# Branch output projection after the fourth unit of the first mixing gate, its first two tiles side by side, and the gated sum split behind all gates

## The chip, the cores and the metric

The kernel runs on one core of a Trainium2 chip. The metric is the device time of one launch in microseconds. Five engines work beside each other and meet at semaphores: TensorE (PE in the profile: matmuls; PEld is its weight loading), VectorE (DVE), ScalarE (ACT), GpSimd (POOL) and SyncE (SP), which here only issues DMAs. Each engine takes its instructions in the order in which the program gives them.

## The reference

Two layers of a hybrid decoder run over 592 tokens (512 prompt tokens, 16 meta tokens, and 8 running sequences of 8). One layer computes, in float32:

```python
proj = rmsnorm(x, ln_g) @ w_in                    # 1024 -> q,k,v,z_a,x_b,z_b,g_a,g_b
o_a = group_norm(retention(q, k, v), gn_g) * silu(z_a)       # 2048 wide, 4 heads
o_b = rglru(causal_conv(x_b)) * silu(z_b)                    # 1536 wide
merged = sigmoid(g_a) * (o_a @ w_a) + sigmoid(g_b) * (o_b @ w_b)
x = x + merged @ w_o
```

After both layers x is normalised once more. The outputs are y and the new retention, convolution and RG-LRU states.

## The kernel before

**Tiles.** Activations lie transposed: a tile is 128 features on the partitions by all 592 tokens. In the last layer the 16 meta tokens are no longer needed, and its later stages work on 576. A product is computed for the two halves of the tokens (296 or 288 columns) in two PSUM banks. Every float32 product is three matmuls (`three`, L1657 to L1659): both operands are split into a high part, which is rounded to the format of the fast matmul, and the low rest; hi·hi, hi·lo and lo·hi are summed. The high part is made by ScalarE as a copy (`w_hi`, `ob_hi`, `xn_hi`), the low part by VectorE as the difference (`w_lo`, `ob_lo`, `xn_lo`).

**Weights.** They come as "units" of 128x1024 (512 KB, eight 128x128 blocks) through a ring of four slots. For each unit SyncE waits until the unit four places earlier is done on TensorE (`unit_done`) and issues the DMA to `w_raw`; ScalarE makes `w_hi` (`split_hi`, L464), VectorE makes `w_lo` in the place of `w_raw` (`split_lo`, L472). `split_hi(ph, i)` and `split_lo(ph, i)` treat the unit three places (`AHEAD`) behind unit i. PSUM banks are a ring of four as well: a job waits for `bank_free` of its bank, and whoever reads the bank sets it free.

**Stages of a layer**, with names as in the code: R (four retention heads, each with its part of `o_a @ w_a` summed into `acc`), L (the RG-LRU branch, whose last work on VectorE are three scans that give the tiles of `ob`, 12 in all), GA (8 units: the projections of the gate g_a), GB (8 units: those of g_b), B (`o_b @ w_b`: 12 units, 8 output tiles m with 12 input tiles k each, 1.5 units to a tile), O (8 units: `merged @ w_o`).

**Around the change.** The order on each engine is written out by hand. In GA and GB ScalarE reads each bank with a tanh into `sg` (`tanh_g`, L934); VectorE multiplies `acc` by the first gate (L1552). Between GA and GB come the splits of `ob` (L990 and L1557). In B VectorE reads each bank itself: it multiplies it by the second gate in `sg` (L1577), adds the tile to `acc` (L1581), and the split of this sum into `xn_hi` (L1002, ScalarE) and `xn_lo` (L1567, VectorE), the operands of O, follows tile by tile. B doesn't read `xn_hi` and `xn_lo`, GA and GB do. O begins with `project_first`, which takes the input tiles k of the sum as they become ready: the first three for one output tile only, and then two output tiles at a time. POOL loads the old x (`xT`, 2368 KB, L688) once `ob` is finished; O adds it. The copy to `xg_hi` in O prepares the next layer.

## Time and profile before

| | us |
|---|---|
| median of 3 runs | 1926.42 (1926.24 to 1926.42) |
| the profiled execution, whole | 1926.77 |
| its span, first to last instruction | 1924.9 |
| TensorE busy in the span | 1904.5 (99%) |
| VectorE, ScalarE, GpSimd busy | 1187.7, 760.9, 267.5 |
| granted TensorE clock, mean | 0.999 of full speed |

The profile's times are from its span's start. L with a number is a line of the kernel before. "Busy" of TensorE contains some overlap of neighbouring matmuls: one is shown with about 0.30 us and the next begins 0.135 us after it. The stages of the first layer that the change touches lie from 736 us (GA begins) to 945 us (in O), and those of the second from 1683 to 1890 us.

### The profile page before, as it was taken

The numbers are of one execution on the slowest core, as the hardware profiler recorded it, in microseconds if no ns is written. First come the engines' busy times: TensorE is split into PE (matmuls) and PEld (weight loads), VectorE is DVE, ScalarE is ACT, GpSimd is POOL, SyncE is SP. The second block draws the span as 40 slices with busy tenths as digits, with TensorE's granted clock in tenths as the row PEclk, the third lists the DMA queues.
The fourth block names the chain that finished last, engine by engine and source line by source line (L and its number), as shares of the span: only waits on it lengthen the run. The fifth ranks groups of instructions, "written<-read, shape, count | busy, mean of one in ns | idle before, by whom it ended". The sixth has DMA issues, their size and how long they took to land.

```text
span 1924.9 us, 32032 instructions
## 1 busy us (share of the span) xinstructions
PE 1904.5 (99%) x13112; PEld 1782.1 (93%) x13112; DVE 1187.7 (62%) x2008; ACT 760.9 (40%) x1181; POOL 267.5 (14%) x375
## 2 busy tenths in 40 slices
PE   8999999999999999999999999999999999999998
PEld 7889898898899999999998988988988999999997
DVE  8775665665766887424487656657557678763345
ACT  5432322323327776422344223233123377754223
POOL 2221120120231200000022201202102422000000
PEclk9999999999999999999999999999999999999999
DMA  6435534453443433322254435534444533342222
GB/s 216 133 117 164 169 136 127 161 174 111 146 149 93 114 99 113 113 77 77 88 172 156 139 127 171 171 114 146 164 127 135 163 102 110 92 138 77 87 79 82
DMA packets 105857, 246.99 MB, mean 128 GB/s; under 512 B 10830, under 2 KB 51262, under 8 KB 105326
## 3 DMA queue, kind: packets, MB, share of 16 engines
q1 hardware_dynamic: 78590, 149.71, 24.9%
q0 software_dynamic: 26976, 95.22, 14.9%
q8 instruction: 104, 1.70, 0.4%
q14 instruction: 43, 0.35, 0.1%
q10 hardware_dynamic: 144, 0.00, 0.0%
HBM read 186.07 MB, written 49.12 MB: 122 GB/s over the span
## 4 chain that ended last, share of the span: by engine, by line
PE 85%; DVE 5%; ACT 4%; DVEq 2%; DMA 1%; ACTq 1%; issue 1%; SPq 0%
PE bank L1657 21%; PE bank L1659 20%; PE bank L1658 20%; PE bank L1727 4%; PE bank L1729 4%; PE bank L1728 4%; PE last L1745 1%; PE last L1727 1%; PE last L1729 1%; PE last L1728 1%; PE sums L1852 1%; PE sums L1854 1%; PE sums L1856 1%; PE bank L1908 1%; PE sums L1763 1%
## 5 line engine op out<-in xcount | busy, mean ns | idle before, releaser
L1657 PE MATMUL bank<-xn_hi,w_hi 128*128 128x296 f32 (+1 forms) x2432 | 726.7, 299 | 0.2
L1659 PE MATMUL bank<-xn_lo,w_hi 128*128 128x296 f32 (+1 forms) x2432 | 722.3, 297 | 0.0
L1658 PE MATMUL bank<-xn_hi,w_lo 128*128 128x296 f32 (+1 forms) x2432 | 721.5, 297 | 0.0
L1657 PEld LDWEIGHTS bank<-xn_hi,w_hi 128*128 128x128 f32 x2432 | 457.3, 188 | 6.6 <-issue 4.3
L1658 PEld LDWEIGHTS bank<-xn_hi,w_lo 128*128 128x128 f32 x2432 | 457.7, 188 | 1.1
L1659 PEld LDWEIGHTS bank<-xn_lo,w_hi 128*128 128x128 f32 x2432 | 456.8, 188 | 0.0
L472 DVE TENSOR_TENSOR w_lo<-w_raw,w_hi 128x1024 fp32r<-128x1024 f32 x245 | 300.3, 1228 | 186.2 <-ACT w_hi L464 179.3
L464 ACT ACTIVATE w_hi<-w_raw 128x1024 fp32r<-128x1024 f32 x245 | 257.8, 1055 | 353.8 <-DMA w_raw<-in_w_units 349.3
L1657 PE MATMUL bank<-oa_hi,w_hi 128*128 128x296 f32 (+1 forms) x512 | 153.7, 300 | 0.0
L1658 PE MATMUL bank<-oa_hi,w_lo 128*128 128x296 f32 (+1 forms) x512 | 151.9, 297 | 0.0
L1659 PE MATMUL bank<-oa_lo,w_hi 128*128 128x296 f32 (+1 forms) x512 | 151.7, 296 | 0.0
L1657 PE MATMUL bank<-ob_hi,w_hi 128*128 128x296 f32 (+1 forms) x384 | 113.9, 297 | 0.0
L1658 PE MATMUL bank<-ob_hi,w_lo 128*128 128x296 f32 (+1 forms) x384 | 113.9, 297 | 0.0
L1659 PE MATMUL bank<-ob_lo,w_hi 128*128 128x296 f32 (+1 forms) x384 | 113.8, 296 | 0.0
L1727 PE MATMUL bank<-w_hi,xn_hi 128*128 128x512 f32 x256 | 100.8, 394 | 0.7 <-DVE rot_k L1191 0.7
L1729 PE MATMUL bank<-w_lo,xn_hi 128*128 128x512 f32 x256 | 100.8, 394 | 0.0
L1728 PE MATMUL bank<-w_hi,xn_lo 128*128 128x512 f32 x256 | 100.7, 393 | 0.0
L1657 PEld LDWEIGHTS bank<-oa_hi,w_hi 128*128 128x128 f32 x512 | 96.3, 188 | 3.9 <-issue 3.9
L1658 PEld LDWEIGHTS bank<-oa_hi,w_lo 128*128 128x128 f32 x512 | 96.3, 188 | 0.0
L1659 PEld LDWEIGHTS bank<-oa_lo,w_hi 128*128 128x128 f32 x512 | 96.3, 188 | 0.0
L606 POOL DMA_DIRECT2D out_ret_s<-S x64 | 46.0, 721 | 326.5 <-DVEq L1142 181.4
L781 ACT ACTIVATE zz<-bank 128x296 f32<-128x296 f32 (+1 forms) x64 | 26.6, 415 | 133.3 <-PE bank L1659 132.7
(293 smaller groups left out, 3069.0 us busy)
## 6 DMA issues: line engine op xcount, KB each, us to landing
w_raw<-in_w_units SPq DMA_DIRECT2D x215, 512.0 KB, 3.6
S<-in_state_ret POOLq DMA_DIRECT2D x64, 512.0 KB, 4.7
out_ret_s<-S POOLq DMA_DIRECT2D x64, 512.0 KB, 6.3
w_raw<-in_w_units SPq DMA_DIRECT2D x66, 256.0 KB, 3.3
vst<-v_scr SPq DMA_DIRECT2D x8, 512.0 KB, 4.0
out_ret_p<-Sp POOLq DMA_DIRECT2D x8, 512.0 KB, 5.7
v_scr<-vtok_hi SPq DMA_DIRECT2D x16, 160.0 KB
dec<-in_decay POOLq DMA_DIRECT2D x9, 264.0 KB, 5.0
```

The lines of the kernel that those rows point to most:

```text
L464: act.activation(w_hi[:, n % RING, :], w_raw[:, n % RING, :], ACT.Copy).then_inc(unit_hi, 1)
L472: dve.tensor_tensor(w_lo[:, n % RING, :], w_raw[:, n % RING, :], w_hi[:, n % RING, :].bitcast(f32), SUB).then_inc(unit_lo, 1)
L606: pool.dma_start(dst, S[:, s, :, :]).then_inc(s_out[s], 16)
L781: act.activation(zz[:, i - 8, a:b], psum_of("R", name)[:, 0:b - a], ACT.Tanh, scale=0.5)\
L1657: pe.matmul(ps, w_hi[:, slot, cols], x_hi, start=first, stop=False)
L1658: pe.matmul(ps, w_lo[:, slot, cols], x_hi, start=False, stop=False)
L1659: return pe.matmul(ps, w_hi[:, slot, cols], x_lo, start=False, stop=last)
L1727: pe.matmul(ps, left_hi, right_hi, start=first, stop=False)
L1728: pe.matmul(ps, left_lo, right_hi, start=False, stop=False)
L1729: return pe.matmul(ps, left_hi, right_lo, start=False, stop=last)
L1745: ins = pe.matmul(o_last[at:at + QUAD, :], qz[:, c, b * QUAD:b * QUAD + QUAD], S[:, s, c, :], start=(n < 4 and c == 0), stop=(n >= 4 and c ...
L1763: return pe.matmul(to[:, :], kst[rows, b // 4, c * P:c * P + P], vst[rows, b // 4, :], start=True, stop=True)
```

## The change

The units now come in the order GA (4 units: g_a tiles 0 to 3), B (12 units), GB (12 units: g_a tiles 4 to 7, then g_b), O. The array of weights in memory stays as it is, and `stored` maps one order to the other.

- TensorE: B begins after the fourth unit of GA. Its output tiles 0 and 1 are computed side by side: for each k, both halves of both tiles, in four banks at once. Units are waited for when their first block is needed.
- ScalarE: the 12 copies `ob_hi` stand behind the third tanh of GA, with the fourth tanh and one weight split behind the first four copies. In B ScalarE copies each bank to `sg`. In GB it writes the tanh to a new buffer `tg` of two tiles. The eight copies `xn_hi` wait for the end of GB.
- VectorE: the differences `ob_lo` come straight behind the last scan and one weight split, and the gates of g_a behind them. In B it only splits weights. In GB it applies both gates and sums. The eight differences `xn_lo` stand behind all of that.
- POOL: the load of `xT` is behind B (its new place in memory is used by `ob` until then).

The diff, without the buffers' new places and the semaphores' names:

```diff
+        def stored(u):
+
+            at = u % UNITS_LAYER
+            first, middle, last = PH["B"].unit0, PH["GB"].unit0, PH["O"].unit0
+            if first <= at < middle:
+                return u + last - middle
+            return u - (middle - first) if middle <= at < last else u
...
-                    sp.dma_start(w_raw[:, u % RING, :], w_units[u]).then_inc(unit_in[u % RING], 16)
+                    sp.dma_start(w_raw[:, u % RING, :], w_units[stored(u)]).then_inc(unit_in[u % RING], 16)
...
-                pool.dma_start(xT[:, :, :].rearrange("p k t -> p (k t)"), x_in if l == 0 else x_scr[l - 1])\
-                    .then_inc(x_again, 16)
                 pool.dma_start(lp[:, :], packs[ds(l + 1, 1)].rearrange("o p w -> (o p) w")).then_inc(lp_in, 16)
...
+                pool.wait_ge(unit_done, l * UNITS_LAYER + PH["B"].after[1])
+                apart(pool)
+                pool.dma_start(xT[:, :, :].rearrange("p k t -> p (k t)"), x_in if l == 0 else x_scr[l - 1])\
+                    .then_inc(x_again, 16)
...
+                def tanh_ga(i):
 
                     for n, (a, b) in enumerate(cut(l)):
                         name = (("proj", i), n)
-                        if ph == "GB":
-                            act.wait_ge(ga_used, l * 16 + it * 8 + (i * 2 + n + 1))
-                        wait_job(act, ph, l, it, name)
+                        wait_job(act, "GA", l, 0, name)
                         apart(act)
-                        act.activation(sg[:, ds(it * 4 + i, 1), a:b].rearrange("p o t -> p (o t)"),
-                                       psum_of(ph, name)[:, 0:b - a], ACT.Tanh, scale=0.5)\
-                           .then_inc(freed(ph, name), 1)
-                        act.drain().then_inc(ga_ready if ph == "GA" else gb_ready, 1)
+                        act.activation(sg[:, i, a:b], psum_of("GA", name)[:, 0:b - a], ACT.Tanh, scale=0.5)\
+                           .then_inc(freed("GA", name), 1)
+                        act.drain().then_inc(ga_ready, 1)
+
+                def tanh_gb(it, i):
+
+                    j = it * 4 + i
+                    for n, (a, b) in enumerate(cut(l)):
+                        name = (("proj", i), n)
+                        if l * 12 + j >= 2:
+                            act.wait_ge(tg_used, (l * 12 + j - 2) * 2 + n + 1)
+                        wait_job(act, "GB", l, it, name)
+                        apart(act)
+                        act.activation(tg[:, j % 2, a:b], psum_of("GB", name)[:, 0:b - a], ACT.Tanh, scale=0.5)\
+                           .then_inc(freed("GB", name), 1)
+                        act.drain().then_inc(tg_ready, 1)
...
-                for ph in ("GA", "GB"):
-                    if ph == "GB":
-                        act.wait_ge(ob_ready, l * LT + LT)
-                        for k in range(LT):
-                            act.activation(ob_hi[:, k, first:], ob[:, k, first:], ACT.Copy).then_inc(obh_ready, 1)
-                    for it in range(0, 2):
-                        for i in range(4):
-                            if (ph, it, i) != ("GA", 0, 0):
-                                tanh_g(ph, it, i)
-                                split_hi(act, ph, l, it, i)
+                def high_ob(k):
+                    act.activation(ob_hi[:, k, first:], ob[:, k, first:], ACT.Copy).then_inc(obh_ready, 1)
+
+                for i in (1, 2):
+                    tanh_ga(i)
+                    split_hi(act, "GA", l, 0, i)
+                act.wait_ge(ob_ready, l * LT + LT)
+                for k in range(4):
+                    high_ob(k)
+                split_hi(act, "GA", l, 0, 3)
+                tanh_ga(3)
+                for k in range(4, LT):
+                    high_ob(k)
                 done = 0
                 for m in range(KT):
                     if m >= 1:
                         split_hi(act, "B", l, 0, done)
                         done += 1
-                    act.wait_ge(mg_ready, l * KT + (m + 1))
-                    act.activation(xn_hi[:, m, first:], acc[:, m, first:], ACT.Copy).then_inc(mgh_ready, 1)
+                    for n, (a, b) in enumerate(cut(l)):
+                        name = (("wb", m), n)
+                        if m < 4:
+                            act.wait_ge(ga_used, l * 8 + m * 2 + n + 1)
+                        wait_job(act, "B", l, 0, name)
+                        act.activation(sg[:, m, a:b], psum_of("B", name)[:, 0:b - a], ACT.Copy)\
+                           .then_inc(freed("B", name), 1)
+                    act.drain().then_inc(gb_in, 1)
                     if m % 2 == 0 or m == KT - 1:
                         split_hi(act, "B", l, 0, done)
                         done += 1
+                for it in range(0, 3):
+                    for i in range(4):
+                        tanh_gb(it, i)
+                        split_hi(act, "GB", l, it, i)
+                act.wait_ge(unit_done, l * UNITS_LAYER + PH["GB"].after[1])
+                for m in range(KT):
+                    act.wait_ge(mg_ready, l * KT + (m + 1))
+                    act.activation(xn_hi[:, m, first:], acc[:, m, first:], ACT.Copy).then_inc(mgh_ready, 1)
...
-
-                for it in range(0, 2):
...
+                split_lo(dve, "GA", l, 0, 2)
+
+                def low_ob(k):
                     dve.wait_ge(obh_ready, l * LT + (k + 1))
                     dve.tensor_tensor(ob_lo[:, k, first:], ob[:, k, first:], ob_hi[:, k, first:].bitcast(f32), SUB)\
                        .then_inc(obl_ready, 1)
...
+                def gate_a(i):
+                    for n, (a, b) in enumerate(cut(l)):
+                        dve.wait_ge(ga_ready, l * 8 + i * 2 + n + 1)
+                        dve.scalar_tensor_tensor(acc[:, i, a:b], sg[:, i, a:b], 1.0, acc[:, i, a:b], ADD, MUL)\
+                           .then_inc(ga_used, 1)
+
+                for k in range(LT):
+                    if k == 4:
+                        split_lo(dve, "GA", l, 0, 3)
+                    low_ob(k)
+                for i in range(4):
+                    gate_a(i)
                 done = 0
+                for m in range(KT):
+                    if m >= 1:
+                        split_lo(dve, "B", l, 0, done)
+                        done += 1
+                    if m % 2 == 0 or m == KT - 1:
+                        split_lo(dve, "B", l, 0, done)
+                        done += 1
...
                 def low_merged(m):
                     dve.wait_ge(mgh_ready, l * KT + (m + 1))
                     dve.tensor_tensor(xn_lo[:, m, first:], acc[:, m, first:], xn_hi[:, m, first:].bitcast(f32), SUB)\
                        .then_inc(mgl_ready, 1)
 
+                for it in range(0, 3):
+                    for i in range(4):
+                        split_lo(dve, "GB", l, it, i)
+                        j = it * 4 + i
+                        m = 4 + i if it == 0 else (it - 1) * 4 + i
+                        for n, (a, b) in enumerate(cut(l)):
+                            dve.wait_ge(tg_ready, (l * 12 + j) * 2 + n + 1)
+                            if it == 0:
+                                dve.scalar_tensor_tensor(acc[:, m, a:b], tg[:, j % 2, a:b], 1.0, acc[:, m, a:b], ADD, MUL)\
+                                   .then_inc(tg_used, 1)
+                            else:
+                                dve.wait_ge(gb_in, l * KT + m + 1)
+                                dve.scalar_tensor_tensor(sg[:, m, a:b], tg[:, j % 2, a:b], 1.0, sg[:, m, a:b], ADD, MUL)\
+                                   .then_inc(tg_used, 1)
+                        if it:
+                            dve.drain()
+                            dve.tensor_tensor(acc[:, m, first:], acc[:, m, first:], sg[:, m, first:], ADD)\
+                               .then_inc(mg_ready, 1)
                 for m in range(KT):
...
-                    for n, (a, b) in enumerate(cut(l)):
-                        if n == 1 and m >= 1:
-                            split_lo(dve, "B", l, 0, done)
-                            done += 1
-                        name = (("wb", m), n)
-                        wait_job(dve, "B", l, 0, name)
-                        dve.scalar_tensor_tensor(sg[:, m, a:b], sg[:, m, a:b], 1.0,
-                                                 psum_of("B", name)[:, 0:b - a], ADD, MUL)\
-                           .then_inc(freed("B", name), 1)
-                    dve.drain()
-                    dve.tensor_tensor(acc[:, m, first:], acc[:, m, first:], sg[:, m, first:], ADD).then_inc(mg_ready, 1)
-                    if m >= 1:
-                        low_merged(m - 1)
-                    if m == KT - 1:
-                        low_merged(m)
-                    if m % 2 == 0 or m == KT - 1:
-                        split_lo(dve, "B", l, 0, done)
-                        done += 1
+                    low_merged(m)
                 dve.wait_ge(x_again, l * 16 + 16)
...
-                for ph in ("GA", "GB"):
-                    for it in range(0, 2):
-                        for i in range(4):
-                            project(ph, l, it, ("proj", i), i)
+                for i in range(4):
+                    project("GA", l, 0, ("proj", i), i)
                 waited = 0
-                for m in range(KT):
-                    while waited * 8 < 12 * (m + 1):
-                        wait_unit("B", l, 0, waited)
-                        waited += 1
-                    for n, (a, b) in enumerate(cut(l)):
-                        name = (("wb", m), n)
-                        wait_bank(pe, "B", l, 0, name)
-                        for k in range(LT):
-                            if m == 0 and n == 0:
+                for ms in ((0, 1), (2,), (3,), (4,), (5,), (6,), (7,)):
+                    for n, k in ([(n, k) for k in range(LT) for n in range(2)] if len(ms) == 2 else
+                                 [(n, k) for n in range(2) for k in range(LT)]):
+                        a, b = cut(l)[n]
+                        for m in ms:
+                            q = 12 * m + k
+                            while waited <= q // 8:
+                                wait_unit("B", l, 0, waited)
+                                waited += 1
+                            name = (("wb", m), n)
+                            if k == 0:
+                                wait_bank(pe, "B", l, 0, name)
+                            if (m, n) == (0, 0):
                                 pe.wait_ge(obl_ready, l * LT + (k + 1))
-                            q = 12 * m + k
                             ins = three(psum_of("B", name)[:, 0:b - a], q // 8 % RING, q % 8,
                                         ob_hi[:, k, a:b], ob_lo[:, k, a:b], k == 0, k == LT - 1)
-                        done("B", name, ins)
+                            if k == LT - 1:
+                                done("B", name, ins)
+                for it in range(0, 3):
+                    for i in range(4):
+                        project("GB", l, it, ("proj", i), i)
```

What this makes of the order of instructions, in the first layer. ScalarE at the end of L and in the gates, before (`sg<-bank` is a tanh of a gate's two halves, `ob_hi<-ob` the copies for B):

```order
L934 ACTIVATE sg<-bank 128x296 x2
L464 ACTIVATE w_hi<-w_raw 128x1024
L990 ACTIVATE ob_hi<-ob 128x592 x12
L934 ACTIVATE sg<-bank 128x296 x2
L464 ACTIVATE w_hi<-w_raw 128x1024
```

The same engine after the change, from the third tanh (L947 is a tanh, L1034 a copy of a bank of B; the first and the second L1034 are tiles 0 and 1):

```order
L947 ACTIVATE sg<-bank 128x296 x2
L477 ACTIVATE w_hi<-w_raw 128x1024
L1012 ACTIVATE ob_hi<-ob 128x592 x4
L477 ACTIVATE w_hi<-w_raw 128x1024
L947 ACTIVATE sg<-bank 128x296 x2
L1012 ACTIVATE ob_hi<-ob 128x592 x8
L1034 ACTIVATE sg<-bank 128x296 x2
L477 ACTIVATE w_hi<-w_raw 128x1024 x2
L1034 ACTIVATE sg<-bank 128x296 x2
L477 ACTIVATE w_hi<-w_raw 128x1024
```

The fourth tanh now has five instructions between it and the third, and the split of B's fourth unit (the first of the two in the eighth row) is behind both copies of tile 0.

TensorE where B begins, after the change, with the waits of each matmul:

```order
L1707 MATMUL bank0<-ob_hi_119,w_hi_51 128x296 [waits obl_ready,bank_free0,unit_lo]
L1708 MATMUL bank0<-ob_hi_119,w_lo_53 128x296
L1709 MATMUL bank0<-ob_lo_118,w_hi_51 128x296
L1707 MATMUL bank1<-ob_hi_119,w_hi_51 128x296 [waits bank_free2,unit_lo]
L1708 MATMUL bank1<-ob_hi_119,w_lo_53 128x296
L1709 MATMUL bank1<-ob_lo_118,w_hi_51 128x296
L1707 MATMUL bank0<-ob_hi_119,w_hi_51 128x296 [waits bank_free1]
```

Three matmuls in, TensorE now waits for the third bank, which holds the first half of GA's fourth unit; before, B's first tile took one bank with 36 matmuls before it turned to the next.

VectorE where the gated sum is finished, before (L1577 gates a half tile of B, L1581 adds it to `acc`, L1595 is in O):

```order
L1577 SCALAR_TENSOR_TENSOR sg<-sg,bank 128x296
L472 TENSOR_TENSOR w_lo<-w_raw,w_hi 128x1024
L1577 SCALAR_TENSOR_TENSOR sg<-sg,bank 128x296
L1581 TENSOR_TENSOR acc<-acc,sg 128x592
L1567 TENSOR_TENSOR xn_lo<-acc,xn_hi 128x592 x2
L472 TENSOR_TENSOR w_lo<-w_raw,w_hi 128x1024
L1595 SCALAR_TENSOR_TENSOR acc<-bank,xT 128x296 x2
```

And after the change:

```order
L1635 TENSOR_TENSOR acc<-acc,sg 128x592
L485 TENSOR_TENSOR w_lo<-w_raw,w_hi 128x1024
L1631 SCALAR_TENSOR_TENSOR sg<-tg,sg 128x296 x2
L1635 TENSOR_TENSOR acc<-acc,sg 128x592
L1616 TENSOR_TENSOR xn_lo<-acc,xn_hi 128x592 x8
L1645 SCALAR_TENSOR_TENSOR acc<-bank,xT 128x296 x2
```

The eight `xn_lo`, six of which were made while B was still running, now stand together behind the last weight split, the last gate and the last sum.

## Rows read from the trace of the kernel before

**Rows 1.** The page: busy time, share and instructions of each engine.

```profile
PE 1904.5 (99%) x13112; PEld 1782.1 (93%) x13112; DVE 1187.7 (62%) x2008; ACT 760.9 (40%) x1181; POOL 267.5 (14%) x375
```

**Rows 2.** By stretch: length, busy PE, PEld, DVE, ACT, POOL; clock, DMA share, GB/s.

```profile
736.00:945.00 209.00, 209.00 (x1540) 209.00 (x1539) 92.00 (x133) 76.60 (x107) 2.22 (x4) 1.00 0.28 93
1683.00:1890.00 207.00, 207.00 (x1561) 206.98 (x1560) 90.97 (x133) 78.27 (x111) 2.22 (x4) 1.00 0.29 95
...
700.00:725.00 25.00, 25.00 (x187) 25.00 (x186) 21.90 (x37) 17.28 (x38) 3.04 (x6) 1.00 0.43 118
...
825.00:850.00 25.00, 25.00 (x186) 25.00 (x185) 4.14 (x4) 5.28 (x8) 0.00 (x0) 1.00 0.19 64
```

**Rows 3.** Waits of TensorE, the largest: total us, times, longest.

```profile
PE bank L1657 <- DVE xg_lo L1063: 1.8, 2, 1.1
```

**Rows 4.** Timeline: start, us, engine, operation; GA's fourth unit ends, a restart.

```profile
761.88 0.30 PE L1659 MATMUL bank<-xn_lo,w_hi 128*128 128x296 f32 x1
...
8.65 1.58 DVE L1063 SCALAR_TENSOR_TENSOR xg_lo<-acc,lp,xg_hi 128x592 fp32r<-128x592 f32 x2 [1.37 <-ACT xg_hi L734]
...
9.54 0.40 PE L1657 MATMUL bank<-xg_hi,w_hi 128*128 128x296 f32 x1 [1.05 <-DVE xg_lo L1063]
```

**Rows 5.** Timeline of ScalarE, first layer: GA's fourth unit, copies of `ob`.

```profile
762.31 0.42 ACT L934 ACTIVATE sg<-bank 128x296 f32<-128x296 f32 x1 [2.85 <-PE bank L1659]
...
789.89 7.15 ACT L990 ACTIVATE ob_hi<-ob 128x592 fp32r<-128x592 f32 x12
```

**Rows 6.** Timeline of VectorE, first layer, last scan and splits.

```profile
762.44 0.77 DVE L1508 SCALAR_TENSOR_TENSOR ob<-rr,ob 128x592 f32<-128x592 f32 x1
...
770.46 1.23 DVE L472 TENSOR_TENSOR w_lo<-w_raw,w_hi 128x1024 fp32r<-128x1024 f32 x1 [1.95 <-ACT w_hi L464]
771.60 0.84 DVE L1552 SCALAR_TENSOR_TENSOR acc<-sg,acc 128x296 f32<-128x296 f32 x2
...
792.08 8.31 DVE L1557 TENSOR_TENSOR ob_lo<-ob,ob_hi 128x592 fp32r<-128x592 f32 x12
```

**Rows 7.** Timelines of ScalarE and VectorE, second layer: fourth unit, last scan.

```profile
1709.81 0.41 ACT L934 ACTIVATE sg<-bank 128x288 f32<-128x288 f32 x1 [2.77 <-PE bank L1659]
...
1710.56 0.75 DVE L1508 SCALAR_TENSOR_TENSOR ob<-rr,ob 128x576 f32<-128x576 f32 x1
```

**Rows 8.** Timelines of ScalarE and VectorE, first layer, GB's end and B.

```profile
840.54 0.42 ACT L934 ACTIVATE sg<-bank 128x296 f32<-128x296 f32 x1 [2.85 <-PE bank L1659]
...
853.85 1.06 ACT L464 ACTIVATE w_hi<-w_raw 128x1024 fp32r<-128x1024 f32 x1 [0.55 <-DMA w_raw<-in_w_units]
...
864.25 1.06 ACT L464 ACTIVATE w_hi<-w_raw 128x1024 fp32r<-128x1024 f32 x1 [2.12 <-DMA w_raw<-in_w_units]
...
842.16 1.23 DVE L472 TENSOR_TENSOR w_lo<-w_raw,w_hi 128x1024 fp32r<-128x1024 f32 x1 [5.29 <-ACT w_hi L464]
...
850.28 0.46 DVE L1577 SCALAR_TENSOR_TENSOR sg<-sg,bank 128x296 f32<-128x296 f32 x1 [4.39 <-PE bank L1659]
...
860.06 0.46 DVE L1577 SCALAR_TENSOR_TENSOR sg<-sg,bank 128x296 f32<-128x296 f32 x1 [3.31 <-PE bank L1659]
860.62 0.77 DVE L1581 TENSOR_TENSOR acc<-acc,sg 128x592 f32<-128x592 f32 x1
861.31 0.77 DVE L1567 TENSOR_TENSOR xn_lo<-acc,xn_hi 128x592 fp32r<-128x592 f32 x1
```

**Rows 9.** Timelines of ScalarE and POOL, a unit that lands late beside xT.

```profile
776.75 1.06 ACT L464 ACTIVATE w_hi<-w_raw 128x1024 fp32r<-128x1024 f32 x1 [0.98 <-DMA w_raw<-in_w_units]
...
763.83 0.58 POOL L688 DMA_DIRECT2D xT<-in_x  x1 [34.15 <-DVE ob L1508]
```

**Rows 10.** End: TensorE's last matmuls, then busy time and clock by microsecond.

```profile
1915.64 0.75 PE L1722 MATMUL sums<-sq,ones 128*128 128x288 f32 x2 [0.59 <-ACT sq L1029]
...
1920.00:1921.00 1.00, 0.00 (x0) 0.00 (x0) 1.00 (x2) 0.00 (x0) 0.00 (x0) 0.86 0.31 115
1921.00:1922.00 1.00, 0.00 (x0) 0.00 (x0) 0.75 (x2) 0.00 (x0) 0.00 (x0) 0.50 1.06 357
```

More of the change, by code:

```diff
@@ L210, in phases @@
     at = (0, 0, 0)
-    for name, passes, units, jobs in (("R", HEADS, 16, r), ("L", 2, 12, l), ("GA", 2, 4, four), ("GB", 2, 4, four),
-                                      ("B", 1, 12, b), ("O", 2, 4, four)):
+    for name, passes, units, jobs in (("R", HEADS, 16, r), ("L", 2, 12, l), ("GA", 1, 4, four), ("B", 1, 12, b),
+                                      ("GB", 3, 4, four), ("O", 2, 4, four)):
         out[name] = Phase(at, passes, units, jobs)
@@ L331, in trunk @@
         xg_hi, xg_lo = Xr["xg_hi"][1], Xr["xg_lo"][1]
-        assert Xr["xg_lo"][0] + KT * T * 4 <= min(R["kst"][0], Mr["xT"][0])
+        assert Xr["xg_lo"][0] + KT * T * 4 <= min(R["kst"][0], b_end)
+        xT = alias("xT", Xr["xg_hi"][0], [P, KT, T])
         trig = alias("trig", R["sc"][0], [P, 2, T])
```

31 lines of the change are left out of this document (10 added, 21 removed).

## The prediction

> **What bounds the kernel now.** I read the page's busy times first. TensorE is busy 1904.5 of 1924.9 us and VectorE, the next, 1187.7 [rows 1], so only what makes TensorE wait or work longer can move the end. Then the stretches that the change touches: from 736 to 945 us and from 1683 to 1890 us TensorE is busy in every microsecond, at full clock [rows 2]. The list of its waits has nothing there either; the largest entry of the whole program is 1.8 us in two waits, for `xg_lo` [rows 3]. So the change can't remove a wait in its own stages. It computes the same products, so TensorE's work stays, and what is left to ask is whether the new order brings waits. For that I follow ScalarE and VectorE instruction by instruction in the timelines of both layers. A wait that arises is paid in full: nothing behind it waits on anything that isn't itself counted from TensorE's own progress, and all of TensorE's idle time in the span is 20.4 us.
>
> **Three measures that all terms use.** (a) A unit's last matmul starts at 761.88; the next matmul would follow 0.135 later, at 762.02, and the reader of the finished bank starts at 762.31 [rows 4, 5]. So the start of a reader is 0.29 after the point from which TensorE's wait counts. (b) The first of two `xg_lo` (1.58 together, so about 0.83 each with some overlap) ends at 9.48, and the matmul that waited for it starts at 9.54: 0.06. It takes 0.40 instead of 0.30, so each restart costs another 0.1 [rows 4]. (c) One matmul in 0.135: 25 us hold 186 of them [rows 2].
>
> **Start of B, first layer.** GA's fourth unit is done for its reader at 762.31 [rows 5]. The last scan's `ob` ends at 762.44 + 0.77 = 763.21 [rows 6], 0.9 later. VectorE then makes a `w_lo` (the next instruction starts 1.14 after it [rows 6]) and the first `ob_lo` (12 in 8.31; one takes 0.77): with 0.08 of overlap, 763.13 + 1.14 + 0.77 = 765.04, and TensorE starts at 765.10. Wait: 765.10 - 762.02 = 3.1. The cover that is gone is large: before, four more units of GA and eight of GB stood here, and `ob_hi` began only at 789.89 [rows 5]. Three matmuls later TensorE needs the third bank, which the fourth tanh sets free. That tanh stands behind four `ob_hi` (12 in 7.15, 0.60 each [rows 5]) and a `w_hi` (1.06 [rows 9], 0.09 of it overlapped), all behind `ob`: 763.25 + 2.4 + 0.97 + 0.42 = 767.0. TensorE would be there at 765.6, so it waits 1.5 more. The fourth bank comes 0.6 after the third, when it is just needed. Sum 3.1 + 1.5 + two restarts = 4.8. From there one k takes TensorE 12 x 0.135 = 1.6, and each splitting engine 0.7 or less: the rest of `ob` is ahead.
> Second layer: `ob` ends at 1710.56 + 0.75 = 1711.31, 1.5 after the reader of the fourth unit at 1709.81 [rows 7], where it was 0.9 in the first. Everything is 0.6 later and a little shorter: 5.3. Together **10.1 us**.
>
> **Behind the pair of tiles.** Tiles 0 and 1 end together, after 144 matmuls. Tile 2 needs B's fourth unit, whose `w_hi` stands behind both copies of tile 0 on ScalarE. The second of these can start 0.4 before the pair's end (three matmuls are behind it). From the start of the last read of a unit's banks to the start of `w_lo` it was 842.16 - 840.54 = 1.62, and `w_lo` takes 1.23 [rows 8]. With the pair's end as 0: -0.4 + 1.62 + 1.23 + 0.06 = 2.5, and by (a) TensorE's wait counts from -0.29: 2.8, with the restart 2.9, twice **5.8 us**. Queued behind that `w_hi` are the fifth unit's and then tile 1's copies; no one waits for these, since tile 3 is 10 us away.
> The fifth unit's slot is set free only at -0.4, because the first three units are now held to the pair's end. After a single release a unit's `w_hi` began 3.57 later (850.28 to 853.85), when two were released together 4.19 (860.06 to 864.25) [rows 8]; `w_hi` and `w_lo` add 2.3. Ready at 5.5 to 6.1, or 6.9 if three transfers together cost the first as much again as two did; TensorE needs it at 2.6 + 24 x 0.135 = 5.8. Cost 0 to 1.1; I take 0.3, near the paired row, twice **0.6 us**.
>
> **End of GB.** Before, `xn_lo` of the last tile was the only one left at B's end, and O's first matmuls used tiles split long ago; there was no wait [rows 2]. Now the eight splits of the sum come after the last gate. With the start of the last tanh as 0: `w_lo` starts at 1.62 [rows 8], the first gate 1.14 later at 2.76, the second 0.38 behind it (two take 0.84 [rows 6]), the sum 0.56 after the second (860.06 to 860.62), the first `xn_lo` 0.69 after the sum (860.62 to 861.31) and takes 0.77 [rows 8]: 5.16, and TensorE starts at 5.22. By (a) it waited from -0.29: 5.5, and 5.6 with the restart; 5.5 in the second layer with its 576 columns. `xn_hi` isn't the last: ScalarE is free for it at about 1.6. Further tiles come every 0.69, and O takes six matmuls, 0.81, to a k at first: no further wait. Together **11.1 us**.
>
> **Costed at nothing.** The bank reads of B move from VectorE to ScalarE, which is 40% busy and has 9.8 us to a tile. `tg` has two tiles, and TensorE takes 13 us for two units, in which VectorE reads them. The load of `xT` now runs beside B's successors: in the trace a unit whose slot was free at about 768.8 was split only at 776.75, 8 us later, while `xT`, issued at 763.83, was under way [rows 9]. The third unit of GB would be ready at 8 + 2.3 = 10.3 after B's end and is needed after two units, 96 x 0.135 = 13.0. If it took 12 instead of 8, that would cost 1.4 to a layer.
>
> **The clock.** TensorE's last matmuls end at 1916.4; the granted clock is 0.86 in the microsecond from 1920 and 0.50 in the next [rows 10], so it fell from 2.4 to 1.2 GHz at about 1920.7, 4.3 us after the last work. The two waits of 5.5 us at GB's end are longer than that, so the clock may fall in them. How soon it comes back no row shows. Bounds: nothing, or as long at half speed as it took to fall, 4.3 us, which is 2.2 us of work lost for each. I take the middle, 1.1, for these two: **2.2 us**; the starts of B (4.6 us with three matmuls in between) could do the same, up to 2.2 each.
> The Trainium skill (TensorE: Matmul & The Clock Gate, Part 1) says that idleness throttles the clock and sustained activity gives it back. By it the clock falls in some of these gaps in each run and the loss is real; without it the sum would be 27.6. The trace agrees on the fall and doesn't show the return.
>
> **Sum.** 10.1 + 5.8 + 0.6 + 11.1 = 27.6, with the clock 29.8. The profiled execution took 1926.77 (span 1924.9 and 1.87 around it), so 1956.6; the median lies 0.35 under that execution: **1956.2 us**.
>
> **Rivals.**
> 1. Only the end of GB costs something: 11.1 + 2.2, so 1939.7. For it speaks that two tiles side by side take 19 us, in which all splits fit. Against it: the splits aren't late as a whole, the first of each is, and `ob` itself ends after GA's fourth unit in both layers [rows 5 to 7]. Chance 0.07.
> 2. The clock falls at the starts of B too and each fall costs the full 2.2 (8.8 in all), and transfers crowd: 0.8 more for each fifth unit and 1.4 for each third unit of GB. 27.6 + 8.8 = 36.4 without the transfers, 1962.8, and 1967 with them. For it: 4.6 us with 0.4 of work is near the 4.3 that sufficed at the end. Against: TensorE does work within that gap, and at the end it did none. Chance 0.10.
> 3. Not slower: TensorE's pace rises. 296 columns at 2.4 GHz are 0.123 us, and a matmul takes 0.1344, perhaps since VectorE reads banks in B meanwhile, which it no longer does. At full pace each matmul gains 0.011; to come within 0.2% takes (27.6 - 3.9) / 0.011, some 2150 matmuls, of the 2304 in B and GB. Against it: with VectorE busy 21.90 of 25 us TensorE started 187 matmuls, with VectorE busy 4.14 it started 186 [rows 2]. Chance 0.02.
> The order of instructions shows that the change does what it says.
>
> **Numbers.** The forecast, with its waits within 10%, has 0.81. Its low end is no clock loss, no wait for the fifth unit and chains a tenth shorter: about 1950.5. Its high end is rival 2 without transfers. Range 1950 to 1963. A change of 0.2% (3.9 us) is what a measurement here can tell. Slower than that 0.95; within it 0.03 (most of rival 3); faster 0.02.
>
> **What would show it.** In the changed profile: TensorE idle about 3 us before B's first matmul, on `ob_lo`, and 1.5 us three matmuls later, on the fourth tanh; about 2.8 us before tile 2, on `w_lo`; about 5.5 us before O, on `xn_lo`; each in both layers; and a granted clock under 1.00 shortly behind the last. Wrong would be: no wait before tile 2 (ScalarE then reached the fourth unit otherwise), waits on transfers in GB (`xT`), or TensorE's idle time under 35 us in all with the time up by more.

## The result and the profile after: 1963.16 us, slower by 1.9%

| | before | after |
|---|---|---|
| median, us | 1926.42 | 1963.16 (1962.63 to 1964.86) |
| ratio of the times, 95% interval | | 1.0191 (1.0174 to 1.0209) |
| profiled execution, us | 1926.77 | 1964.86 |
| its span | 1924.9 | 1963.1 |
| granted TensorE clock, mean | 0.999 | 0.992 |

The direction was right, and every wait that was forecast at over half a microsecond is there, to within 0.4 us. The forecast of 1956.2 is 7.0 short and the range, which ended at 1963.0, doesn't hold the time: what follows the waits on TensorE's clock was worth 9.8 us and not 2.2. The page of the profile after, its span and busy times, answers to [rows 1]:

```profile
span 1963.1 us, 32120 instructions
PE 1917.5 (98%) x13112; PEld 1793.5 (91%) x13112; DVE 1185.7 (60%) x2008; ACT 772.5 (39%) x1213; POOL 267.6 (14%) x375
```

TensorE is "busy" for 13 us more, with the same 13112 matmuls, and idle for 25 more. The idle part first. The list of TensorE's waits, total us, times and longest, answers to [rows 3]:

```profile
PE bank L1707 <- DVE xn_lo L1616: 10.8, 2, 5.4
PE bank L1707 <- DVE ob_lo L1590: 6.9, 2, 3.9
PE bank L1707 <- DVE w_lo L485: 5.2, 2, 2.6
PE bank L1707 <- ACT sg L947: 2.5, 2, 1.3
PE bank L1707 <- DVE xg_lo L1105: 2.1, 3, 1.3
```

The first four entries are new and make 25.4 us, in eight waits of which each stands once in each layer. The fifth was the largest before. The rows of these waits on TensorE, first layer, with the wait in brackets:

```profile
765.80 0.38 PE L1707 MATMUL bank<-ob_hi,w_hi 128*128 128x296 f32 x1 [2.99 <-DVE ob_lo L1590]
...
767.71 0.59 PE L1707 MATMUL bank<-ob_hi,w_hi 128*128 128x296 f32 x1 [1.27 <-ACT sg L947]
...
791.13 0.53 PE L1707 MATMUL bank<-ob_hi,w_hi 128*128 128x296 f32 x1 [2.60 <-DVE w_lo L485]
...
935.30 0.58 PE L1707 MATMUL bank<-xn_hi,w_hi 128*128 128x296 f32 x1 [5.42 <-DVE xn_lo L1616]
935.68 0.45 PE L1708 MATMUL bank<-xn_hi,w_lo 128*128 128x296 f32 x1
935.92 0.45 PE L1709 MATMUL bank<-xn_lo,w_hi 128*128 128x296 f32 x1
...
941.53 0.30 PE L1708 MATMUL bank<-xn_hi,w_lo 128*128 128x296 f32 x1
941.67 0.30 PE L1709 MATMUL bank<-xn_lo,w_hi 128*128 128x296 f32 x1
```

At 765.80 B's first matmul, for the first `ob_lo`; three matmuls later 767.71, for the fourth tanh; 791.13 tile 2, for the fourth unit's `w_lo`; 935.30 O, for `xn_lo`. The last rows show the rest of the loss. From 935.68 to 941.11 one matmul starts 0.247 us after the other (22 steps), and behind 941.53 it is 0.135 again. The same in busy time by stretch, columns as in [rows 2], where the clock was 1.00 throughout:

```profile
736.00:762.00 26.00, 26.00 (x194) 26.00 (x193) 16.86 (x31) 20.68 (x28) 0.00 (x0) 1.00 0.19 62
767.80:770.80 3.00, 3.00 (x13) 3.00 (x14) 2.81 (x4) 2.89 (x6) 0.00 (x0) 0.51 0.02 9
791.30:794.60 3.30, 3.30 (x14) 3.30 (x15) 1.32 (x2) 2.73 (x4) 0.00 (x0) 0.50 0.69 263
935.30:941.30 6.00, 6.00 (x24) 6.00 (x25) 4.64 (x7) 0.98 (x2) 0.00 (x0) 0.50 0.00 0
941.50:947.50 6.00, 6.00 (x46) 6.00 (x45) 0.00 (x0) 0.00 (x0) 0.00 (x0) 1.00 0.00 0
1734.20:1740.00 5.80, 5.80 (x24) 5.80 (x25) 5.62 (x8) 5.11 (x9) 0.00 (x0) 0.50 0.01 3
1897.90:1903.90 6.00, 6.00 (x25) 6.00 (x26) 4.43 (x7) 0.83 (x2) 0.00 (x0) 0.50 0.01 3
```

GA's first 26 us are as before, 26.00 busy at clock 1.00. Each of the five stretches at 0.50 lies behind a new wait and is counted as busy, with 24 or 25 matmuls in 6 us, 13 in 3, where the stretch from 941.50 has 46 in 6. They make most of the 13 us of more "busy" time. Between them TensorE worked 24.8 us at half speed; each of these microseconds does only 0.135/0.247 of its work, so 0.455 of it is lost, 11.3 us. Of the six places with a wait of over 2.5 us only tile 2 in the second layer kept the full clock.

How ScalarE and VectorE came to be late, at B's start on ScalarE and at GB's end on VectorE (start, us, engine, operation):

```profile
763.86 2.46 ACT L1012 ACTIVATE ob_hi<-ob 128x592 fp32r<-128x592 f32 x4 [5.30 <-DVE ob L1550]
766.23 1.04 ACT L477 ACTIVATE w_hi<-w_raw 128x1024 fp32r<-128x1024 f32 x1
767.17 0.39 ACT L947 ACTIVATE sg<-bank 128x296 f32<-128x296 f32 x1
```

```profile
931.62 1.23 DVE L485 TENSOR_TENSOR w_lo<-w_raw,w_hi 128x1024 fp32r<-128x1024 f32 x1 [3.66 <-ACT w_hi L477]
932.76 0.83 DVE L1631 SCALAR_TENSOR_TENSOR sg<-tg,sg 128x296 f32<-128x296 f32 x2
933.69 0.78 DVE L1635 TENSOR_TENSOR acc<-acc,sg 128x592 f32<-128x592 f32 x1
934.38 2.82 DVE L1616 TENSOR_TENSOR xn_lo<-acc,xn_hi 128x592 fp32r<-128x592 f32 x4
```

These are the rows from which the terms were built, in their new order: `ob` done at 763.83, four `ob_hi`, one `w_hi` and the tanh behind them [rows 5, 6]; `w_lo`, two gates, the sum and the first `xn_lo`, 934.38 + 0.77 = 935.15 [rows 8].

### The profile page after: what moved, and what is told of

Same layout as the page of the kernel before. It is cut to its first block, busy times and chain, and to the rows that moved or that the text cites. A ratio compares the mean times of both kernels' runs of the same rounds, so it can differ in the third digit from the quotient of the medians.

```text
span 1963.1 us, 32120 instructions
## 1 busy us (share of the span) xinstructions
PE 1917.5 (98%) x13112; PEld 1793.5 (91%) x13112; DVE 1185.7 (60%) x2008; ACT 772.5 (39%) x1213; POOL 267.6 (14%) x375
## 4 chain that ended last, share of the span: by engine, by line
PE 83%; DVE 6%; ACT 5%; DVEq 2%; ACTq 1%; issue 1%; DMA 1%; SPq 0%
PE bank L1707 20%; PE bank L1709 20%; PE bank L1708 20%; PE bank L1777 4%; PE bank L1779 4%; PE bank L1778 4%; PE last L1795 1%; PE last L1777 1%; PE last L1779 1%; PE last L1778 1%; DVE rr L1544 1%; DVE w_lo L485 1%; PE sums L1902 1%; PE bank L1958 1%; PE sums L1906 1%
## 5 line engine op out<-in xcount | busy, mean ns | idle before, releaser
L1707 PE MATMUL bank<-xn_hi,w_hi 128*128 128x296 f32 (+1 forms) x2432 | 729.5, 300 | 10.9 <-DVE xn_lo L1616 10.8
L1707 PEld LDWEIGHTS bank<-ob_hi,w_hi 128*128 128x128 f32 x384 | 74.7, 195 | 15.9 <-DVE w_lo L485 12.9
```

Of the source, the lines that this page charges most:

```text
L1707: pe.matmul(ps, w_hi[:, slot, cols], x_hi, start=first, stop=False)
```

## The experiments

Each is the changed kernel with one edit, if nothing else is said. The four of a group ran on one chip beside its own runs of the kernel before: medians 1927.21 us (1925.68 to 1927.98) for the first group and 1926.27 (1925.10 to 1928.04) for the second. "Over before" is the median less that one; for the changed kernel it was 36.7 us.

| run | edit | us | ratio to before | over before |
|---|---|---|---|---|
| e1_busy | matmuls of a constant in the waits | 1953.48 | 1.0140 (1.0124 to 1.0155) | 26.3 |
| e2_tanh4 | fourth tanh first | 1959.46 | 1.0171 (1.0156 to 1.0186) | 32.3 |
| e3_unit4 | fourth unit split earlier | 1962.04 | 1.0184 (1.0167 to 1.0201) | 34.8 |
| e4_merge | six split pairs before the last gate | 1955.50 | 1.0148 (1.0133 to 1.0163) | 28.3 |
| e5_nopair | tiles 0 and 1 in turn | 1957.93 | 1.0162 (1.0147 to 1.0177) | 31.7 |
| e7_after8 | B behind all eight units of GA | 1949.98 | 1.0120 (1.0103 to 1.0136) | 23.7 |
| e8_mended | e2, e3 and e4 together | 1948.69 | 1.0113 (1.0098 to 1.0128) | 22.4 |
| e9_after8_mended | e7, e5 and e4 together | 1932.44 | 1.0029 (1.0018 to 1.0040) | 6.2 |

### e1_busy: is it the clock?

```diff
+                def busy(n):
+                    for _ in range(n):
+                        pe.matmul(sums[0][:, 0:P], ones[:, :], ones[:, :], start=True, stop=True)
+                pe.wait_ge(gate_free, 6 * GROUPS * (l + 1))
+                busy((12, 15)[l])
...
+                            if (n, k) == (0, 0) and m in (1, 2):
+                                busy((5, 10)[m - 1])
...
+                    if it == 0:
+                        busy(22)
```

> The changed kernel, with matmuls of the constant `ones` (128x128, written to a PSUM bank that nothing reads then) put where TensorE waits: 12 or 15 before B's first matmul, 5 before the fourth matmul group's bank, 10 before tile 2, 22 before O. Each takes 0.23 us in the trace, so every group ends before its wait does and moves nothing. Theory A (what the sum lacked is the clock: TensorE ran at 1.2 GHz for 24.8 us of work in five stretches behind the new waits, where a matmul takes 0.247 instead of 0.135): granted clock 1.00 until the last matmul, the waits' ends unchanged, and 0.455 x 24.8 = 11.3 us less, 1952 us. Theory B (the fall goes with the waits but the lost time is elsewhere, in later waits or transfers): clock 1.00, and the time stays within 2 us of 1963.

Measured 1953.48, 9.8 us less by the ratios (1.0191 to 1.0140) and 10.4 by the distances to before. The waits that are left on the same three releasers, where the matmuls of `ones` don't reach:

```profile
PE bank L1707 <- DVE xn_lo L1616: 1.0, 2, 0.5
PE bank L1707 <- DVE ob_lo L1590: 0.8, 2, 0.5
PE bank L1707 <- DVE w_lo L485: 0.7, 2, 0.4
```

O's start, where the 22 of them (each f32 matmul is two records) fill all but 0.51 us, and the two stretches behind O's starts in both layers:

```profile
925.64 5.07 PE L2033 MATMUL sums<-ones 128*128 128x128 f32 x44
931.22 0.37 PE L1707 MATMUL bank<-xn_hi,w_hi 128*128 128x296 f32 x1 [0.51 <-DVE xn_lo L1616]
931.43 0.29 PE L1708 MATMUL bank<-xn_hi,w_lo 128*128 128x296 f32 x1
```

```profile
931.00:937.00 6.00, 5.78 (x42) 5.81 (x43) 4.88 (x8) 1.21 (x3) 0.00 (x0) 1.00 0.01 3
1889.00:1895.00 6.00, 5.79 (x44) 5.82 (x45) 4.74 (x8) 1.14 (x2) 0.00 (x0) 1.00 0.01 3
```

O's matmuls follow each other at full pace at once, and the clock stays at 1.00 to the last matmul. The waits still end where they did: from where a matmul behind GA's last would start (0.135 us after it) to the start of B's last it takes 85.8 us in the first layer, 78.2 before the change and 88.7 after it, where 1.4 and 1.6 of half speed are contained. Theory A holds. The 11.3 us were worked out from the changed kernel's profiled execution, which was 1.7 us above its median; between the two profiled executions, 1964.86 and 1953.52, the distance is 11.3. What e1 has over before, 26.3 us, is the price of the waits alone; the forecast's sum for these was 27.6.

### e2_tanh4: the fourth tanh's place

```diff
+                tanh_ga(3)
                 act.wait_ge(ob_ready, l * LT + LT)
                 for k in range(4):
                     high_ob(k)
                 split_hi(act, "GA", l, 0, 3)
-                tanh_ga(3)
```

> The changed kernel with ScalarE's fourth tanh of GA before the copies of `ob` instead of behind four of them and a weight split. My step: the second wait at B's start (1.27 and 1.24 us) is this tanh's place alone, and goes: 2.5 + two restarts = 2.7 us less, 1960.4 us, or up to 4 less again where the clock's fall at B's start goes with it. The first wait (3.0, 3.9) stays or grows by under 0.1. Rival: B's start waits for whatever comes last in ScalarE's and VectorE's row anyway, and the wait moves to the second `ob_lo`: 1963 us.

4.4 us less. The waits on `sg` are gone from the list, and the others stand as they were:

```profile
PE bank L1707 <- DVE ob_lo L1590: 6.9, 2, 3.9
PE bank L1707 <- DVE w_lo L485: 5.2, 2, 2.6
```

The waits didn't move elsewhere. The gain is 1.7 us over the 2.7, and the clock isn't shown to be all of that. In its profile the low clock lasted 3.4 us at B's start in the second layer, where it had lasted 6.8, but it also fell behind tile 2's wait in the second layer, where it had stayed up:

```profile
1755.30:1758.60 3.30, 3.30 (x16) 3.30 (x15) 2.45 (x2) 1.84 (x4) 0.00 (x0) 0.50 0.31 127
```

From B's start on TensorE worked 23.2 us at half speed instead of 24.8, which is worth 0.7 us of the 4.0 between the two profiled executions. The other 3.3 are 0.6 more than the forecast for the wait, within the 1 to 2.2 us by which the executions of one kernel (the changed one, e1 to e3) differ.

### e3_unit4: the fourth unit's place

The loop over `n` in this cut holds the copies of tile m.

```diff
                 for m in range(KT):
-                    if m >= 1:
-                        split_hi(act, "B", l, 0, done)
-                        done += 1
+                    split_hi(act, "B", l, 0, done)
+                    done += 1
                     for n, (a, b) in enumerate(cut(l)):
...
-                    if m % 2 == 0 or m == KT - 1:
+                    if m >= 1 and m % 2 == 0 or m == KT - 1:
```

> The changed kernel with the split of B's fourth unit on ScalarE before the copies of tile 0 instead of behind them. Theory A: the wait before tile 2 (2.6 us in each layer) goes and comes back 24 matmuls later, at the fifth unit: its slot is set free only at the pair's end, its data land 3.2 us behind that and are split 2.35 later, where TensorE arrives 3.2 behind the end; 2.2 us of wait, so 0.3 us to a layer less and 1962.5 us. Theory B: the place of that split is the cause: both waits go, 5.2 us and the half-speed stretch behind one of them (1.5) less, 1956.4 us.

1.9 us less by the distance to before, 1.3 by the ratios, whose intervals overlap: A, and not B with 6.7. ScalarE waits for the fifth unit's data with nothing left to do before it, and TensorE reaches that unit after tile 2's first 24 matmuls and waits there:

```profile
788.78 0.42 ACT L1033 ACTIVATE sg<-bank 128x296 f32<-128x296 f32 x1 [0.40 <-PE bank L1708]
792.18 1.06 ACT L477 ACTIVATE w_hi<-w_raw 128x1024 fp32r<-128x1024 f32 x1 [2.99 <-DMA w_raw<-in_w_units]
```

```profile
794.55 0.40 PE L1706 MATMUL bank<-ob_hi,w_hi 128*128 128x296 f32 x1 [2.21 <-DVE w_lo L485]
```

The wait is 2.21 instead of 2.60, and 2.33 in the second layer. ScalarE's order isn't the only cause: with it mended, the pair still holds three units to its end, so that their slots are refilled too late. Without the pair (e5, below) no wait on `w_lo` is left there.

### e4_merge: what O's start waits for

```diff
-                        split_hi(act, "GB", l, it, i)
+                        if (it, i) != (2, 3):
+                            split_hi(act, "GB", l, it, i)
...
                 for m in range(KT):
+                    if m == 6:
+                        split_hi(act, "GB", l, 2, 3)
...
-                        split_lo(dve, "GB", l, it, i)
+                        if (it, i) != (2, 3):
+                            split_lo(dve, "GB", l, it, i)
+                        else:
+                            for k in range(6):
+                                low_merged(k)
...
-                for m in range(KT):
+                split_lo(dve, "GB", l, 2, 3)
+                for m in (6, 7):
                     low_merged(m)
```

> The changed kernel with six of the eight pairs `xn_hi`, `xn_lo` before the last gate, the last sum and the last weight split (on ScalarE that split is behind six `xn_hi`). My step: TensorE's wait before O is the row w_lo, two gates, sum, xn_lo; without the first four it starts at 0.53 + 0.70 + 0.77 + 0.1 = 2.1 us behind the last tanh's start instead of 5.3: wait 2.2 instead of 5.4, 6.4 us less in both layers. If a wait of 2.2 leaves the clock up (one of 2.6 did and one didn't), another 5.6 less: 1951 us; if the clock falls as before, 1957 us. Rival: O's first matmuls wait for the last sum all the same, and the time stays at 1963 us.

8.4 us less. Its two waits before O on TensorE, the rows of VectorE there, and the stretches behind O's starts:

```profile
PE bank L1715 <- DVE xn_lo L1619: 4.7, 2, 2.4
```

```profile
930.06 4.21 DVE L1619 TENSOR_TENSOR xn_lo<-acc,xn_hi 128x592 fp32r<-128x592 f32 x6 [3.36 <-ACT xn_hi L1050]
934.18 0.84 DVE L1638 SCALAR_TENSOR_TENSOR sg<-tg,sg 128x296 f32<-128x296 f32 x2
```

```profile
930.00:936.00 6.00, 5.01 (x37) 5.04 (x38) 5.84 (x10) 4.58 (x9) 0.00 (x0) 1.00 0.19 74
1887.00:1893.00 6.00, 5.68 (x43) 5.71 (x44) 5.91 (x10) 4.46 (x7) 0.00 (x0) 1.00 0.14 55
```

The first `xn_lo` no longer stands behind `w_lo`, gates and sum, and O waits 4.7 in two instead of 10.8: the chain was the cause. The waits are 2.36 and 2.32 where 2.2 was expected, and 6.1 us less in both layers where 6.4 was. The four runs were 1951.69, 1953.95, 1957.06 and 1958.21, spread over 6.5 us where the runs of e1 spread over 1.6. In the profiled one, the fastest, the clock stayed up behind both of these waits.

### e10_merge_again, e11_merge_third, e12_merge_fourth: the spread of e4

The kernel of e4 unchanged, three more executions with a trace each, beside one execution of the kernel before at 1926.59 us.

> The kernel of e4 once more, for a second trace. Its four runs lay from 1951.7 to 1958.2 us. Theory A: the spread is the clock, which falls behind O's waits of 2.3 us in some executions; then the time less 0.455 us for each microsecond of work at half speed is the same as in e4's first trace, where 10.9 us of work ran at half speed and the execution took 1951.7. Theory B: the spread has another source, such as transfers; then the times differ with the same half-speed work.

> As the run before, a third trace of the same kernel: theory A expects (time - 0.455 x work at half speed) within 1 us of the other two.

> As the two runs before, a fourth trace of the same kernel, with the same expectation of theory A.

| execution | us | span | work at half speed, us | of it in the first 15 us | span less 0.455 x the rest |
|---|---|---|---|---|---|
| e4 | 1951.69 | 1949.8 | 12.6 | 0 | 1944.1 |
| e12 | 1952.31 | 1950.5 | 12.6 | 0 | 1944.8 |
| e10 | 1954.79 | 1953.0 | 24.3 | 6.5 | 1944.9 |
| e11 | 1957.59 | 1955.8 | 27.9 | 3.4 | 1944.6 |

The work at half speed is TensorE's busy time inside the stretches with a clock of 0.50 (the 10.9 us of the expectation were miscounted and are 12.6). With all of it subtracted the four spans still differ by 2.8 us, so the 1 us of theory A fails as it was written. With the stretches of the first 15 us left out, where TensorE waits for x and the first units anyway, they agree within 0.8. That was left out only after the numbers were seen, but the traces bear it out: the first matmul behind TensorE's wait of 1.6 us for `qk` starts at 27.07 in e4 and 27.45 in e12, at 27.06 in e11, with 3.4 us of half speed before it, and at 27.80 in e10, with 6.5, which by 0.455 would have cost 3.0. So the spread is the clock to within 0.8 us, and half speed cost little where TensorE was fed slowly anyway. Behind O's start in e11, the stretch that was at 1.00 in e4:

```profile
932.70:935.90 3.20, 3.20 (x15) 3.20 (x14) 3.20 (x7) 3.06 (x5) 0.00 (x0) 0.50 0.02 9
```

The same reckoning brings the changed kernel's profiled span from 1963.1 to 1951.8, and e1, which has no half speed, has 1951.7.

### e5_nopair: side by side or in turn

```diff
-                for ms in ((0, 1), (2,), (3,), (4,), (5,), (6,), (7,)):
+                for ms in ((0,), (1,), (2,), (3,), (4,), (5,), (6,), (7,)):
```

> The changed kernel with B's tiles 0 and 1 one after the other, like the others; the rest as changed. Theory A (what costs at B's start is that the splits of `ob` begin late, whatever the order of matmuls): TensorE's first half tile needs a new `ob_lo` every 0.405 us and VectorE makes one in 0.69, with the weight split, the copies and the tanh on ScalarE between: 7.5 us of waits in small pieces in the first layer and 8.1 in the second, and in return no wait for the fourth tanh and none before tile 2 (together 4.0 and 4.0 us in the trace, with restarts 4.4). Waits 15.6 instead of 14.6 in both layers, so +1; how much the clock falls in a stretch that is half busy is open, between none (5.6 us less than the changed kernel's loss at B) and the same: 1958 to 1965 us. Theory B (side by side is what costs, since it holds three units to the pair's end): 1963 - 5.2 - 2.5 = 1955 us.

1957.93, just below A's range and above B's number, so neither expectation holds as written; what the waits show is A's mechanism. The waits of over 0.15 us are few, and the stretch from 768 to 774, in B's first half tile, is at half clock:

```profile
PE bank L1707 <- DVE ob_lo L1590: 8.7, 4, 3.9
```

```profile
768.00:774.00 6.00, 5.01 (x20) 4.65 (x20) 5.81 (x9) 4.87 (x9) 0.00 (x0) 0.50 0.00 0
```

The small waits were there in another form: at half speed TensorE takes 0.74 us for a k, about as long as VectorE for an `ob_lo`, so it lost nothing by the clock that it wouldn't have waited. By the measure used for e1, B takes 85.8 us in the first layer here, which is what e1 took with the pair and at full clock; in the second both take 84.7. So side by side and in turn cost the same in B when the clock's loss is left aside, 7.6 us over before in the first layer. The pair turns many small waits into whole ones, the one at its end among them, and the half speed behind these comes on top: as it runs, the kernel with the pair is 5.0 us slower (36.7 over before against 31.7).

### e7_after8, e8_mended, e9_after8_mended: do the parts add up?

The first puts B back behind all of GA; the core of it (the loops and counts of the engines, which follow from it, are left out):

```diff
-    for name, passes, units, jobs in (("R", HEADS, 16, r), ("L", 2, 12, l), ("GA", 1, 4, four), ("B", 1, 12, b),
-                                      ("GB", 3, 4, four), ("O", 2, 4, four)):
+    for name, passes, units, jobs in (("R", HEADS, 16, r), ("L", 2, 12, l), ("GA", 2, 4, four), ("B", 1, 12, b),
+                                      ("GB", 2, 4, four), ("O", 2, 4, four)):
```

> The place of B alone undone: B stands behind all eight units of GA instead of four, the pair side by side and the sum behind all gates stay. Theory A (each part costs its own waits, by the sum): the waits at B's start (3.0, 1.3, 3.9, 1.2) go with their half-speed stretches (1.4 and 2.7): the splits of `ob` have 26 us of cover more. Left are 2.6 before tile 2 and 5.4 before O, in both layers, 16.0 + 1.1 for restarts and pipeline, and 6 to 9 for the clock: 1951 us. Rival (the wait at B's start is not its place but the four banks taken at once): the wait for the last tanh stays with about 0.5 to 1.3 us, 1953 us and a visible wait on sg.

> The changed kernel with three repairs of the order, each alone measured or in this set: the fourth tanh first, the fourth unit's split before the copies of tile 0, six split pairs of the sum before the last gate. If the parts add up: waits of 3.0 and 3.9 at B's start, 2.3 in tile 2 and 2.3 before O, 16.1 us in six, 1.6 for restarts, and the clock 3 to 6: 1927 + 17.7 + 4.5 = 1949 us. If the repairs share their gain (the clock's fall is one for several waits), more than 1953.

> B behind all eight units of GA, no tiles side by side, the sum's splits as in the run before (six pairs before the last gate); what is left of the change is the gated sum behind all gates, with copies of B's banks on ScalarE. By the sum only the wait before O remains, 2.3 us in each layer and 0.5 for both restarts, with the clock perhaps falling once: 1927 + 5.2 = 1932 us, up to 1935. Rival (ScalarE's copies of B's banks or the buffer tg cost something by themselves, hidden in the other runs): over 1936 us.

1949.98, 1948.69 and 1932.44, for 1951, 1949 and 1932 expected. The largest entries of TensorE's waits, in this order:

```profile
PE bank L1700 <- DVE xn_lo L1615: 10.8, 2, 5.4
PE bank L1700 <- DVE w_lo L485: 5.2, 2, 2.6
PE bank L1700 <- DVE qk L1227: 1.6, 1, 1.6
```

```profile
PE bank L1714 <- DVE ob_lo L1592: 6.8, 2, 3.9
PE bank L1714 <- DVE xn_lo L1618: 4.7, 2, 2.4
PE bank L1714 <- DVE w_lo L485: 4.5, 2, 2.3
```

```profile
PE bank L1708 <- DVE xn_lo L1618: 4.7, 2, 2.4
PE bank L1708 <- DVE qk L1230: 1.7, 1, 1.7
```

With eight units of GA ahead of B nothing waits at its start, not even for the fourth bank. e9 keeps only the sum behind all gates: 4.7 us of waits in two, and 6.2 over before. Its copies of B's banks on ScalarE and the buffer `tg` cost nothing that can be seen. No version of this order comes below the kernel before, which has no wait in these stages to lose.

## Why the prediction was wrong, point by point

**What bounds the kernel: right.** Hardly anything of the waits was given back: the gaps, 0.165 for each of the eight (explained in the next point) and their restarts make 25.4 + 1.3 + 0.8 = 27.5, and e1 has 26.3 over before. By that measure the sum for the waits, 27.6, was 1.3 too high, which hid a part of what the clock was priced too low.

**Start of B: right.** 3.1 and 1.5 us were forecast for the first layer by the distance to the natural next start. The gaps shown are 2.99 and 1.27, and they begin at the end of a matmul's shown 0.30, 0.165 later than that measure: 3.15 and 1.44. Second layer 5.3 forecast, 4.02 + 1.41 and two restarts measured, 5.6. The orders shown ahead of the prediction are said to have five instructions between the third and the fourth tanh; there are six, of which five stand behind `ob`, and with those five the sum was made.

**Behind the pair: right**, 2.9 forecast for each, 2.60 + 0.17 + 0.1 measured. The fifth unit, 0.3 forecast, cost nothing here: its `w_lo` ended at 793.95, and at full clock TensorE would have come to it at 791.13 + 0.1 + 3.2 = 794.4. By e3 the arrival of the data is nearly as late as ScalarE's row for tile 2.

**End of GB: right**, 5.6 and 5.5 forecast, 5.42 and 5.36 shown, 5.68 and 5.62 with both additions. e4 took `w_lo`, the gates and the sum out of the chain together, and the waits fell by 3.06 and 3.04; no run took out a single link.

**Costed at nothing: right.** No wait on a transfer arises in GB, and e9 bounds the new copies and `tg`.

**The clock: the step that failed.** The forecast put it as "I take the middle, 1.1, for these two: 2.2 us; the starts of B (4.6 us with three matmuls in between) could do the same, up to 2.2 each". Measured, it is 9.8 us (e1 against the changed kernel). In the profiled execution the 11.3 us divide as follows: 5.6 behind O's two starts, where the sum had 2.2; 4.1 behind B's two starts and 1.6 behind one wait before tile 2, where it had nothing. Both factors were too small. First the number: the clock fell at five of six places, at B's start in both layers, before tile 2 in the first, and at both of O's starts. The row it rested on, 4.3 us from TensorE's last matmul to the fall [rows 10], was read as the time that a wait must last. The waits of 2.60 before tile 2 show that this is no measure: behind one of two the clock fell. Second the size: behind O's start six microseconds of work ran at half speed, at 0.247 instead of 0.135 for a matmul, which is 2.8 us for one fall. The upper bound of 2.2 was "as long at half speed as it took to fall", a guess at the return from a row of the fall. The range's high end was four falls at that bound, 8.8 us; the profiled execution had five, at 1.4 to 2.8.

The Trainium skill (TensorE: Matmul & The Clock Gate, Part 1) was named there with the rule that idleness throttles the clock and sustained activity gives it back. The traces agree with both halves, 0.50 behind the waits and 1.00 again from 941.50 on. In all ten cases of a wait of 5.4 us before O (this run, e2, e3, e5, e7) the clock fell.

**The rivals.** The second came closest: 1962.8 without the transfers, at a chance of 0.10. It had the falls at B's starts right and none before tile 2, and its 2.2 for a fall was too low for O and for B in the second layer, and too high for B in the first, so its near hit is in part luck. The first and third have nothing for them: B's start cost 10 us, and in e9, where B's banks are read by ScalarE too, B took 78.2 us as before. The 0.03 for no change can't be "most of rival 3", which had 0.02.

## What to carry to other kernels

Where TensorE has no idle time, a reordering of the same work has nothing to win, and the waits that it brings can be read, here to 0.3 us each, from the durations of the rows that the new order puts in front of the first matmul: take each engine's row in order, not its busy share. Put matmuls of a constant into a wait that can't be avoided, or count the lost pace on top of it: here nothing or about 1.5 us behind single waits of 2.2 to 2.6 us, and 1.4 to 2.8 behind those of 5.4. Computing two output tiles side by side to cover a late operand also holds their weight slots and banks to the common end; here it saved nothing in waits over one tile after the other, and was 5.0 us slower by what the clock did.

## What the runs showed of the hardware that was not expected

- A wait of 2.60 us was enough for the granted clock to fall from 2.4 to 1.2 GHz, in one layer and not in the other with the same wait. Over all profiles with such a wait before tile 2 it fell in 10 of 14 cases, between 0.1 us before the wait's end and 1.5 us behind it; behind waits of 2.36 and 2.32 before O (e4, e8 to e12) in 4 of 12; and behind waits of 2.20 to 2.33 in tile 2 (e3, e8) in one of 4, that of 2.20. TensorE had been busy without a break before each. So one kernel, e4's, has runs that differ by 6.5 us.
- Behind O's start (5.4 us idle) the low clock lasted 6.1 us into the work; over the ten such starts it was 3.0 to 6.2 us of work. A matmul of 296 columns took 0.247 us from start to start then, and 0.135 at full clock: 1.83 times as long.
- Constant matmuls that filled the waits to within 0.5 us kept the clock at 1.00 in all eight places, and gave back 9.8 us of 36.7.
- At the half clock TensorE lost little or nothing where it was fed at that pace anyway: e5 with the half clock in B's first half tile takes 85.8 us for B, as e1 at full clock; e11, with 3.4 us of half speed in the kernel's first 15, comes to its matmul at 27.06 us as early as e4 (27.07) without.
